# The second layer's modulation blocks move from TensorE to VectorE

## The chip, the cores and the metric

The kernel runs on one core of one Trainium2 chip. The metric is the device time of one execution in microseconds (us), the median of the runs shown. TensorE multiplies matrices into eight PSUM banks, VectorE and ScalarE do elementwise work, SyncE only issues the loads of the weights. Everything lies in fp32; a large product is made of three fp32r products of a rounded high part and a remainder.

## What is computed

The reference is two blocks of two transformer layers on 512 tokens (and 256 context tokens in the first) of 1024 features. For the change the first block's modulation and its first feed-forward part matter:

```
sh1, sc1, g1, sh2, sc2, g2 = ada_modulation(c, w_ada[i], b_ada[i])            # the same for c_ctx
h = modulate(x, norm_mix[i], sh1, sc1)
...
x = x + g2[:, None, :] * conv_ffn(modulate(x, norm_ffn[i], sh2, sc2),
                                  ffn_w_up[i], ffn_conv_w[i], ffn_conv_b[i], ffn_w_down[i])

def conv_ffn(h, w_up, conv_w, conv_b, w_down):
    u = depthwise_conv3(h @ w_up, conv_w, conv_b)
    a, g = jnp.split(u, 2, axis=-1)
    return (jax.nn.silu(g) * a) @ w_down
```

The modulation of layer i is silu(c) and silu(c_ctx), each a vector of 1024, times w_ada[i] (1024 x 6144), plus a bias. It is cut into twelve blocks c of 512 columns. Those of the second layer (i = 1) are needed only from the end of the first feed-forward part on.

## The kernel before

Features lie on partitions, tokens along them: a tile is 128 features by 256 tokens (context) or 512 (main), the "small" and the "large" tile. Each engine runs a list written out by hand, with waits on counts of the others' work (pe_done, act_done, dve_done).

**Weights.** All weights pass a ring of four slots of 128 x 2048 in the order of the list `plan`. SyncE issues the load of piece i when the piece i - 4 has been used: released by VectorE for the pieces that are split, by TensorE for the others. A split piece is rounded by ScalarE (L354, WH), and VectorE takes the remainder (L362, WL); there are two buffers for that, so piece k waits for TensorE to be done with piece k - 2. Up weights are 1 MB in two transfers of 512 KB, down weights 768 KB a half, modulation weights 1 MB a half.

**The stage a0** (the first feed-forward stage, `conv_ffn_*` and `ffn_pe` with the tag "a0") has 22 up blocks j in groups of three (the last group has one). Up group 0 runs first, then up group g and down group g - 1 alternate, and down group 7 ends it. An up block is 2 parts x 2 tiles x 8 x 3 matmuls (`up_pe`, L400) into four banks. ScalarE takes them out with the middle tap of the convolution (L1293), VectorE adds the two others (L1314, L1318), ScalarE applies Silu (L1299), VectorE multiplies (L1325), ScalarE rounds the result (L1273) and VectorE takes its remainder (L1279). A down group is 8 pairs of a small and a large tile of 9 matmuls each (`down_pe`), and VectorE adds each tile to X (L1369). `take` hands out six PSUM banks in turn; a bank is free when its last reader is done. Behind the last down group's tiles a norm follows (L530, L519, L582, L568).

**The modulation blocks of the second layer** hang on the odd up blocks (`extra`, ada1_pe, ada1_act, ada1_dve). `ada_pe` makes 16 products of 256 columns (L627, printed as 32 records) of the weights with the two conditions in the stationary place, in four quarters of the rows of one bank; ScalarE copies the bank to `spare` (L643); `ada_turn_pe` (L635) turns and adds it with four products of two columns (8 records), and VectorE adds the bias (L649). Block 10 stands behind up block 21, and behind it block 11 and the turns of 10 and 11.

Of the kernel before, what the change touches and what calls it, by code (L numbers as in the profile page):

```python
# [109 lines left out]
def build(nc, io, counts):  # L110
    known = counts.known
    ctx = ExitStack()
    with ctx:
# [11 lines left out]
        sel = sb("sel", [P, 2])  # L125
        modv = sb("modv", [P, 2, 48, 2])
# [93 lines left out]
        plan = []  # L220
        GATE_ORDER = [(0, 0), (2, 0), (1, 0), (0, 1), (2, 1), (1, 1)]
# [9 lines left out]
        def weights_list():  # L231
            def ada(l, c):
                pieces(("ada", l, c), io["w_ada"][l], 512 * c, 512 * c + 512)

            for c in range(4):
                ada(0, c)
            g_in = io["gla_w_in"][0]
            for h in range(GLA_H):
                piece((("gla_in", h), 0), [(0, cols(g_in, h * 128, h * 128 + 128)),
                                           (128, cols(g_in, 512 + h * 128, 640 + h * 128))])  # L240
                piece((("gla_in", h), 1), [(0, cols(g_in, 1024 + h * 256, 1280 + h * 256))])
                ada(0, 4 + 2 * h)
# [5 lines left out]
            def ffn(tag, up, down, extra):  # L248
                def ups(g):
                    for j in range(GROUP * g, min(GROUP * g + GROUP, FT)):  # L250
                        piece(("up", tag, j), [(0, cols(up, 128 * j, 128 * j + 128)),
                                               (128, cols(up, FF + 128 * j, FF + 128 * j + 128))], True)
                        if j % 2:
                            extra(j // 2)

                def downs(g):
                    rows = down[128 * GROUP * g:128 * min(GROUP * g + GROUP, FT), :]
                    pieces(("down", tag, g), rows, 0, D, True, 512)

                for g in range(-(-FT // GROUP)):  # L260
                    ups(g)
                    if g:
                        downs(g - 1)
                downs(FT // GROUP)

            def ada1(c):
                ada(1, c)
                if c == FT // 2 - 1:
                    ada(1, c + 1)

            ffn("a0", io["ffn_w_up"][0], io["ffn_w_down"][0], ada1)
# [10 lines left out]
            ffn("a1", io["ffn_w_up"][1], io["ffn_w_down"][1], lambda c: None)  # L282
            for l in range(2):
                w = io["w_in_2"][l]
                piece(("idx", l, 0), [(0, cols(w, 4608, 4864))], True)

                piece(("idx", l, 1), [(0, cols(w, 4864, 4928)), (64, cols(w, 4864, 4932))], True)
                for b in (0, 2, 1):
                    for n in range(3):
                        c0 = 1536 * b + 512 * n  # L290
                        pieces(("in", l, b, n), w, c0, c0 + 512, True)
                for b, c in GATE_ORDER:
                    u = ("w_up_a_2", "w_up_b_2", "w_up_c_2")[b]
                    for i in range(2):
# [8 lines left out]
                ffn(f"b{l}", io["w_gu_2"][l], io["w_down_2"][l], lambda c: None)  # L303

        weights_list()
        where = {}
# [190 lines left out]

        def residual_tiles(spec):
# [11 lines left out]
        def square_act(spec, i):  # L510
# [4 lines left out]
            if i >= 2:  # L515
                nc.scalar.wait_ge(pe_done, at(("hsq_read", key, i - 2)))
            elif ("ada_turned", 1, 10 + i) in counts.at and key == "n1":
                nc.scalar.wait_ge(pe_done, at(("ada_turned", 1, 10 + i)))
# [120 lines left out]
        def ada_act(l, c):  # L639
            nc.scalar.wait_ge(pe_done, at(("ada", l, c)))  # L640
            if c >= 2:
                nc.scalar.wait_ge(pe_done, at(("ada_turned", l, c - 2)))
            nc.scalar.copy(ada_rows[:, c % 2, :], bank_of(("ada", l, c))).then_inc(  # L643
                act_done, mark("act", ("ada_rows", l, c), ("free", ("ada", l, c))))

# [130 lines left out]
        def start_dve():  # L776
            nc.vector.memset(eps[:, :], EPS).then_inc(dve_done, mark("dve", ("eps",)))
            nc.vector.memset(cond[:, :, :], 0.0).then_inc(dve_done, mark("dve", ("cond0",)))
# [431 lines left out]
        GROUPS = -(-FT // GROUP)  # L1210

        def group(g):
            return range(GROUP * g, min(GROUP * g + GROUP, FT))

        def up_pe(tag, groups, g, extra, spec):
            for j in group(g):
# [13 lines left out]
                if j % 2:  # L1230
                    extra(j // 2)
# [8 lines left out]
        def down_pe(tag, groups, g, spec):  # L1240
# [19 lines left out]
        def ffn_pe(tag, groups, extra, spec, out_spec):  # L1260
            for g in range(GROUPS + 1):
                if g < GROUPS:
                    up_pe(tag, groups, g, extra, spec)
# [19 lines left out]
        def conv_act(tag, l, groups, g, extra):  # L1283
            for j in group(g):
# [16 lines left out]
                if j % 2:  # L1301
                    extra(j // 2)

        def conv_dve(tag, l, groups, g, extra):
            for j in group(g):
                split_dve(after(("up", tag, j)))
                for part in range(2):
                    t = 22 * part + j
                    for t0, tn in groups if j else reversed(groups):
# [10 lines left out]
                            ALU.mult, ALU.add).then_inc(dve_done, mark("dve", ("conv", tag, j, part), ("free", key)))  # L1320
                nc.vector.wait_ge(act_done, at(("silu", tag, j)))
# [6 lines left out]
                if j % 2:  # L1328
                    extra(j // 2)
# [43 lines left out]
        def down_dve(tag, groups, g, gate, spec):  # L1373
            for i in range(2):
                split_dve(after((("down", tag, g), i)))
                for n in range(4 * i, 4 * i + 4):
                    for t0, tn in groups:
                        down_tile_add_dve(tag, g, n, t0, tn, gate, spec)

# [36 lines left out]
        def conv_ffn_act(tag, l, groups, extra, spec):  # L1416
            for g in range(GROUPS + 1):
                if g < GROUPS:
                    conv_act(tag, l, groups, g, extra)
# [5 lines left out]
        def conv_ffn_dve(tag, l, groups, gate, extra, spec):  # L1425
            for g in range(GROUPS + 1):
                if g < GROUPS:
                    conv_dve(tag, l, groups, g, extra)
# [1313 lines left out]
        def ada1_pe(c):  # L2742
            ada_pe(1, c)
            if c:
                ada_turn_pe(1, c - 1)
            if c == FT // 2 - 1:
                ada_pe(1, c + 1)
                ada_turn_pe(1, c)
                ada_turn_pe(1, c + 1)

        def ada1_act(c):
            ada_act(1, c)
            if c == FT // 2 - 1:
                ada_act(1, c + 1)

        def ada1_dve(c):
            if c:
                ada_dve(1, c - 1)
            if c == FT // 2 - 1:
                ada_dve(1, c)  # L2760
                ada_dve(1, c + 1)

        def nothing(c):
            pass

# [22 lines left out]
        def _(pe):  # L2788
# [8 lines left out]
            residual_pe("gla_out", lambda k, t0, tn: Y[:, k, t0:t0 + tn], ALL, hnorms["n0f"],  # L2797
                        passes=[(("gla_out", CTX), ALL[1:]), (("gla_out", 0), ALL[:1])])
            ffn_pe("a0", ALL, ada1_pe, hnorms["n0f"], hnorms["n1"])
# [4 lines left out]
            ffn_pe("a1", MAIN, nothing, hnorms["n1f"], hnorms["m", 0])  # L2804
            for l in range(2):
# [16 lines left out]
                ffn_pe(f"b{l}", MAIN, nothing, hnorms["f", l], hnorms["final"] if l else hnorms["m", 1])  # L2822

        @block.scalar
        def _(act):
# [11 lines left out]
            conv_ffn_act("a0", 0, ALL, ada1_act, hnorms["n1"])  # L2837
# [6 lines left out]
            conv_ffn_act("a1", 1, MAIN, nothing, hnorms["m", 0])  # L2844
# [26 lines left out]
        def _(dve):  # L2871
# [11 lines left out]
            conv_ffn_dve("a0", 0, ALL, mod_gate(0, 1), ada1_dve, hnorms["n1"])  # L2883
# [6 lines left out]
            conv_ffn_dve("a1", 1, MAIN, mod_gate(1, 1), nothing, hnorms["m", 0])  # L2890
# [88 lines left out]
```

## Time and profile before

| | us |
|---|---|
| median of 3 runs | 4456.69 |
| lowest, highest | 4453.78, 4457.04 |
| the profiled execution | 4463.18 |
| its span | 4461.4 |
| TensorE busy in the span | 4143.4 (93%) |
| VectorE busy | 1902.6 (43%) |
| ScalarE busy | 1359.2 (30%) |
| mean granted clock of TensorE | 0.959 of full |

The profile lists instructions by source line. Times are counted from the span's start. "L400 x96" are 96 records of line 400; "[0.91 <-ACT conv L1299]" is idle time of the engine ahead of an instruction, and what ended it. The chain follows the work that ended last back from the end, at each step to what released it.

### The profile page before, as it was taken

How to read it: one execution, taken by the hardware profiler on the slowest of the kernel's cores; microseconds unless marked ns; L12 is line 12 of the kernel's file. 1: busy time of each engine (PE TensorE's matmuls, PEld its weight loads, DVE VectorE, ACT ScalarE, POOL GpSimd, SP SyncE). 2: the span in 40 equal slices, each digit the busy share in tenths (PEclk: the TensorE clock that was granted, in tenths of full speed). 3: DMA queues.
4: the chain of work that ended last, by engine and by line, in shares of the span. 5: the costliest groups of instructions: out<-in, count | busy, mean ns of one | idle time of the engine just before them, and what ended most of it. 6: DMA issues, size and time to landing. Idle time of an engine off the chain costs nothing.

```text
span 4461.4 us, 47797 instructions
## 1 busy us (share of the span) xinstructions
PE 4143.4 (93%) x19512; PEld 3053.1 (68%) x19512; DVE 1902.6 (43%) x2995; ACT 1359.2 (30%) x2239; POOL 16.9 (0%) x33
## 2 busy tenths in 40 slices
PE   7999889999988999999888999899988889998999
PEld 3676548888865556887756666588866665656887
DVE  1333115544442325655475531343437754224334
ACT  2222124222234424333133332332222334323222
POOL 0000000000000000000000000000000000000000
PEclk9898999999989999999889999999989999999999
DMA  4232023323220012333111112233232111222331
GB/s 152 67 92 69 29 65 110 109 88 108 89 82 16 26 36 80 96 99 94 60 57 41 55 57 85 69 92 98 82 93 67 50 48 32 82 88 77 96 95 62
DMA packets 385175, 333.51 MB, mean 75 GB/s; under 512 B 12416, under 2 KB 351872, under 8 KB 384832
## 3 DMA queue, kind: packets, MB, share of 16 engines
q1 hardware_dynamic: 382384, 319.09, 23.6%
q0 software_dynamic: 2576, 11.37, 0.8%
q8 instruction: 157, 2.57, 0.2%
q14 instruction: 58, 0.48, 0.0%
HBM read 328.34 MB, written 2.10 MB: 74 GB/s over the span
## 4 chain that ended last, share of the span: by engine, by line
PE 73%; DVE 7%; ACT 5%; issue 2%; DMA 0%; ACTq 0%; DVEq 0%
PE ps L400 53%; PE ps L411 3%; PE ps L413 3%; PE ps L412 3%; PE ps L530 2%; DVE WL L362 1%; ACT WH L354 1%; PE ps L2041 1%; ACT arena_m L1706 1%; PE ps L1666 1%; PE ps L2019 1%; DVE arena_m L1688 1%; DVE arena_m L1683 1%; PE ps L599 1%; PE ps L600 1%
## 5 line engine op out<-in xcount | busy, mean ns | idle before, releaser
L362 DVE TENSOR_TENSOR WL<-ring,WH 128x2048 fp32r<-128x2048 f32 (+3 forms) x221 | 461.3, 2088 | 356.7 <-ACT WH L354 356.4
L354 ACT CAST WH<-ring 128x2048 fp32r<-128x2048 f32 (+3 forms) x221 | 384.1, 1738 | 478.0 <-PE ps L400 386.9
L400 PE MATMUL ps<-MH,WH 128*128 128x512 f32 x1024 | 399.9, 391 | 3.2 <-DVE WL L362 3.2
L400 PE MATMUL ps<-ML,WH 128*128 128x512 f32 x1024 | 399.7, 390 | 0.0
L400 PE MATMUL ps<-MH,WL 128*128 128x512 f32 x1024 | 399.5, 390 | 0.0
L411 PE MATMUL ps<-MH,WH 128*128 128x512 f32 x768 | 344.4, 448 | 13.1 <-DVE WL L362 13.1
L400 PE MATMUL ps<-IH,WH 128*128 128x512 f32 (+1 forms) x880 | 336.9, 383 | 0.0
L400 PE MATMUL ps<-IL,WH 128*128 128x512 f32 (+1 forms) x880 | 325.8, 370 | 0.0
L400 PE MATMUL ps<-IH,WL 128*128 128x512 f32 (+1 forms) x880 | 325.1, 369 | 0.0
L413 PE MATMUL ps<-MH,WL 128*128 128x512 f32 x768 | 310.2, 404 | 0.0
L412 PE MATMUL ps<-ML,WH 128*128 128x512 f32 x768 | 309.8, 403 | 0.0
L400 PE MATMUL ps<-arena_m,ring 128*128 128x512 f32 x640 | 286.0, 595 | 3.3 <-issue 3.3
L400 PE MATMUL ps<-HH,WH 128*128 128x512 f32 (+1 forms) x728 | 246.5, 339 | 0.0
L400 PE MATMUL ps<-HL,WH 128*128 128x512 f32 (+1 forms) x728 | 245.6, 337 | 0.0
L400 PE MATMUL ps<-HH,WL 128*128 128x512 f32 (+1 forms) x728 | 245.1, 337 | 0.0
L400 PEld LDWEIGHTS ps<-MH,WH 128*128 128x128 f32 x1024 | 192.9, 188 | 43.9 <-DVE WL L362 3.6
L400 PEld LDWEIGHTS ps<-ML,WH 128*128 128x128 f32 x1024 | 192.9, 188 | 40.3
L400 PEld LDWEIGHTS ps<-MH,WL 128*128 128x128 f32 x1024 | 192.9, 188 | 40.1
L400 PEld LDWEIGHTS ps<-arena_m,ring 128*128 128x128 f32 x640 | 121.7, 191 | 138.6 <-issue 134.9
L411 PEld LDWEIGHTS ps<-MH,WH 128*128 128x128 f32 x768 | 150.6, 196 | 85.9 <-issue 44.4
L400 PE MATMUL ps<-H,ring 128*128 128x256 f32 (+1 forms) x512 | 185.0, 518 | 10.8 <-ACT arena_a L1123 10.8
L1293 ACT ACTIVATE conv<-ps,vec 128x512 f32<-128x512 f32 (+1 forms) x132 | 92.4, 705 | 321.0 <-PE ps L400 315.4
(289 smaller groups left out, 6808.0 us busy)
## 6 DMA issues: line engine op xcount, KB each, us to landing
ring<-in_w_in SPq DMA_DIRECT2D x62, 1024.0 KB, 5.2
ring<-in_w_ada SPq DMA_DIRECT2D x48, 1024.0 KB, 8.6
ring<-in_ffn_w_up SPq DMA_DIRECT2D x88, 512.0 KB, 5.2
ring<-in_w_gu SPq DMA_DIRECT2D x88, 512.0 KB, 5.1
ring<-in_ffn_w_down SPq DMA_DIRECT2D x28, 768.0 KB, 4.5
ring<-in_w_down SPq DMA_DIRECT2D x28, 768.0 KB, 4.4
ring<-in_gla_w_in SPq DMA_DIRECT2D x8, 1024.0 KB, 9.5
ring<-in_gla_w_out SPq DMA_DIRECT2D x8, 1024.0 KB, 5.0
```

The lines of the kernel that those rows point to most:

```text
L354: nc.scalar.copy(split_slot(key, WH), raw_slot(key)).then_inc(act_done, mark("act", ("rounded", k)))
L362: nc.vector.tensor_tensor(split_slot(key, WL), raw_slot(key), split_slot(key, WH).bitcast(F32), ALU.subtract).then_inc(dve_done, mark("dve ...
L400: m = nc.tensor.matmul(out, l, r, start=(i == 0), stop=(i == len(pairs) - 1))
L411: nc.tensor.matmul(out, lh, rh, start=first and i == 0, stop=False)
L412: nc.tensor.matmul(out, lh, rl, start=False, stop=False)
L413: m = nc.tensor.matmul(out, ll, rh, start=False, stop=end)
L530: m = nc.tensor.matmul(ps[:, bank, 0:tn], mat("mean1024"), NSQ[:, i % 2, 0:tn], start=(n == 0), stop=(n == DT - 1))
L599: nc.tensor.matmul(out, wh, xh, start=(k == 0), stop=False)
L600: nc.tensor.matmul(out, wl, xh, start=False, stop=False)
L1293: nc.scalar.activation(conv[:, j % 2, part, t0:t0 + tn], bank_of(key)[:, 0:tn], ACT.Identity, scale=v("conv_w", 132 * l + 44 + t), bias=v( ...
L1666: m = nc.tensor.matmul(out[64 * e:64 * e + 64, 0:P], it["v"](k)[:, 64 * e:64 * e + 64], pt[:, e, 128 * k:128 * k + 128], start=(k == 0), s ...
L1683: nc.vector.tensor_tensor(probs(i), src, bias, ALU.add).then_inc(dve_done, mark("dve", (name, "biased", i), *[("free", (name, "s", i, e)) ...
```

## The change

The twelve modulation blocks of the second layer leave TensorE. VectorE multiplies each 128 x 512 tile k (0 to 7) of a block's weights by the condition's value of that row and adds it up in `spare`, for the two conditions (s = 0, 1): one TENSOR_SCALAR for k = 0, a SCALAR_TENSOR_TENSOR for each other k (`ada_part_dve`). TensorE then sums the 128 partitions with eight products of one column against a tile of ones (`ada_sum_pe`). The pieces of weights are cut by rows (tiles 0 to 3 and 4 to 7, 512 columns) and their slots are released by VectorE. Blocks 0, 1, 3, 5, 7, 9, 11 lie in up groups 0 to 6 (tiles 0-2, 3-5 and 6-7 in the three up blocks), blocks 2, 4, 6, 8, 10 in down groups 0 to 4 (one tile behind each pair of additions). The sums of the blocks from the ups stand behind the fourth tile of the next down group on TensorE, those from the downs behind the first up block of the next group.

```diff
@@ weights_list
             def ffn(tag, up, down):
                 def ups(g):
                     for j in group(g):
                         piece(("up", tag, j), [...], True)
-                        if j % 2:
-                            extra(j // 2)
+                        if tag == "a0" and g in ADA_UP and j % GROUP < 2:
+                            ada_rows_of(ADA_UP[g], j % GROUP)
                 def downs(g):
-                    pieces(("down", tag, g), rows, 0, D, True, 512)
+                    for i in range(2):
+                        piece((("down", tag, g), i), [(0, cols(rows, 512 * i, 512 * i + 512))], True)
+                        if tag == "a0" and g in ADA_DOWN:
+                            ada_rows_of(ADA_DOWN[g], i)
@@
+        def ada_part_dve(c, ks):
+            if ks[0] == 0:
+                if c == 0:
+                    for t0 in (0, CTX):
+                        nc.vector.wait_ge(pe_done, at(("hms", "n0f", t0)))
+                else:
+                    nc.vector.wait_ge(pe_done, at(("ada_turned", 1, c - 1)))
+                    ada_dve(1, c - 1)
+            for k in ks:
+                key = (("ada", 1, c), k // 4)
+                n, loads_n = where[key]
+                nc.vector.wait_ge(slot_loaded[n % SLOTS], loads_n)
+                x = raw_slot(key).rearrange("p (t n) -> p t n", n=512)[:, k % 4, :]
+                for s in range(2):
+                    acc = ada_sums[:, s, :]
+                    if k == 0:
+                        m = nc.vector.tensor_scalar(acc, x, cond[:, k, s:s + 1], None, ALU.mult)
+                    else:
+                        nc.vector.wait_ge(dve_done, at(("ada_part", c, k - 1, s)))
+                        m = nc.vector.scalar_tensor_tensor(acc, x, cond[:, k, s:s + 1], acc, ALU.mult, ALU.add)
+                    m.then_inc(dve_done, mark("dve", ("ada_part", c, k, s), *([used(key)] if k % 4 == 3 else []),
+                                              *([("ada_sum", c)] if k == DT - 1 else [])))
+
+        def ada_sum_pe(c):
+            nc.tensor.wait_ge(dve_done, at(("ada_sum", c)))
+            out = take(("ada_turned", 1, c))
+            for j in range(4):
+                for s in range(2):
+                    m = nc.tensor.matmul(out[:, 2 * j + s:2 * j + s + 1], ada_sums[:, s, 128 * j:128 * j + 128], ones[:, :],
+                                         start=True, stop=True)
+            m.then_inc(pe_done, mark("pe", ("ada_turned", 1, c)))
@@ up_pe
-                if j % 2:
-                    extra(j // 2)
+                if tag == "a0" and j % GROUP == 0 and j and g - 1 in ADA_BEFORE_UP:
+                    ada_sum_pe(ADA_BEFORE_UP[g - 1])
@@ down_pe
                     done += 1
+                    if tag == "a0" and done == 4 and g in ADA_BEFORE_DOWN:
+                        ada_sum_pe(ADA_BEFORE_DOWN[g])
@@ conv_dve, behind the two convolution instructions of the block's last tile
+                if tag == "a0" and g in ADA_UP:
+                    ada_part_dve(ADA_UP[g], ((0, 1, 2), (3, 4, 5), (6, 7))[j % GROUP])
                 nc.vector.wait_ge(act_done, at(("silu", tag, j)))
@@ down_dve
                     for t0, tn in groups:
                         down_tile_add_dve(tag, g, n, t0, tn, gate, spec)
+                    if tag == "a0" and g in ADA_DOWN:
+                        ada_part_dve(ADA_DOWN[g], (n,))
@@ block.sync
-                if i >= SLOTS and plan[i - SLOTS][2]:
+                if i >= SLOTS and (plan[i - SLOTS][2] or plan[i - SLOTS][0] in summed_pieces):
                     sp.wait_ge(dve_done, at(("slot_used", i - SLOTS)))
```

**SyncE's queue from up block 7 to up block 9, around down group 1.** `in_w_ada` are modulation weights, `in_ffn_w_up` and `in_ffn_w_down` the up and down weights; in brackets is the engine that releases the slot. Before:

```order
L2780 DMA ring<-in_ffn_w_up 128x8x128 [waits pe_done]
L2780 DMA ring<-in_ffn_w_up 128x8x128
L2780 DMA ring<-in_w_ada 128x8x256 [waits dve_done] x2
L2780 DMA ring<-in_ffn_w_up 128x8x128 [waits dve_done]
L2780 DMA ring<-in_ffn_w_up 128x8x128
L2780 DMA ring<-in_ffn_w_down 128x3x512 [waits dve_done]
L2780 DMA ring<-in_ffn_w_down 128x3x512 [waits pe_done]
L2780 DMA ring<-in_ffn_w_up 128x8x128 [waits pe_done]
L2780 DMA ring<-in_ffn_w_up 128x8x128
```

After:

```order
L2808 DMA ring<-in_ffn_w_up 128x8x128 [waits dve_done]
L2808 DMA ring<-in_ffn_w_up 128x8x128
L2808 DMA ring<-in_w_ada 128x4x512 [waits dve_done]
L2808 DMA ring<-in_ffn_w_up 128x8x128 [waits dve_done]
L2808 DMA ring<-in_ffn_w_up 128x8x128
L2808 DMA ring<-in_ffn_w_down 128x3x512 [waits dve_done]
L2808 DMA ring<-in_w_ada 128x4x512 [waits dve_done]
L2808 DMA ring<-in_ffn_w_down 128x3x512 [waits dve_done]
L2808 DMA ring<-in_w_ada 128x4x512 [waits dve_done]
L2808 DMA ring<-in_ffn_w_up 128x8x128 [waits dve_done]
L2808 DMA ring<-in_ffn_w_up 128x8x128
```

The halves of a modulation block now stand apart, one behind each of two up weights and one behind each half of the down weights, and every slot is released by VectorE.

**VectorE from the third up block of a group into the first pairs of the down group.** `conv` is the convolution's result, `WL` the remainder of the weights, `spare` the sums of a modulation block, `modv` its result. Before:

```order
L1314 SCALAR_TENSOR_TENSOR conv<-ps,vec,conv 128x511
L1318 SCALAR_TENSOR_TENSOR conv<-ps,vec,conv 128x511
L1325 TENSOR_TENSOR conv<-conv 128x768
L1279 TENSOR_TENSOR IL<-conv,IH 128x768
L649 TENSOR_TENSOR modv<-ps,vec 128x4 x2
L362 TENSOR_TENSOR WL<-ring,WH 128x1536
L1369 SCALAR_TENSOR_TENSOR X<-ps,modv,X 128x256
L1369 SCALAR_TENSOR_TENSOR X<-ps,modv,X 128x512
L1369 SCALAR_TENSOR_TENSOR X<-ps,modv,X 128x256
L1369 SCALAR_TENSOR_TENSOR X<-ps,modv,X 128x512
```

After:

```order
L1362 SCALAR_TENSOR_TENSOR conv<-ps,vec,conv 128x511
L1366 SCALAR_TENSOR_TENSOR conv<-ps,vec,conv 128x511
L680 SCALAR_TENSOR_TENSOR spare<-ring,cond,spare 128x512 x4
L1375 TENSOR_TENSOR conv<-conv 128x768
L1329 TENSOR_TENSOR IL<-conv,IH 128x768
L372 TENSOR_TENSOR WL<-ring,WH 128x1536
L1417 SCALAR_TENSOR_TENSOR X<-ps,modv,X 128x256
L1417 SCALAR_TENSOR_TENSOR X<-ps,modv,X 128x512
L697 TENSOR_TENSOR modv<-ps,vec 128x4 x2
L677 TENSOR_SCALAR spare<-ring,cond 128x512 x2
L1417 SCALAR_TENSOR_TENSOR X<-ps,modv,X 128x256
L1417 SCALAR_TENSOR_TENSOR X<-ps,modv,X 128x512
```

Four instructions (tiles 6 and 7 of a block) stand ahead of the product of the up block, and two behind each pair of additions.

**TensorE behind the second pair of a down group**, where the sum stands now:

```order
L410 MATMUL ps<-IH,WH 128x512
L410 MATMUL ps<-IL,WH 128x512
L410 MATMUL ps<-IH,WL 128x512
L690 MATMUL ps<-ones,spare 128x1 x8
L410 MATMUL ps<-IH,WH 128x256
L410 MATMUL ps<-IL,WH 128x256
L410 MATMUL ps<-IH,WL 128x256
```

Before, no down group held anything but its own products; the modulation products stood behind odd up blocks.

## Rows read from the trace of the kernel before

**Rows 1.** The page, part 1: busy time and share of the span by engine.

```profile
PE 4143.4 (93%) x19512; PEld 3053.1 (68%) x19512; DVE 1902.6 (43%) x2995; ACT 1359.2 (30%) x2239; POOL 16.9 (0%) x33
```

**Rows 2.** The chain in order of time: start us, length us, what; stage a0.

```profile
698.75 16.69 PE ps L400 x96
...
1169.81 58.59 PE ps L400 x336
1229.45 4.46 DMA ring<-in_ffn_w_down
...
1248.86 27.55 PE ps L400 x144
```

**Rows 3.** Busy time in a stretch: us, DVE busy, clock, DMA share, GB/s.

```profile
698.00:1228.00 530.00, 262.14 (x354) 1.00 0.33 99
```

**Rows 4.** The chain from 985 to 1075 us, around a modulation block.

```profile
1007.78 1.86 PE ps L627 x32
1009.64 0.98 PE ps L635 x8
1010.63 58.59 PE ps L400 x336
```

**Rows 5.** TensorE behind up block 21: start, us, line; in brackets idle before.

```profile
1228.32 1.93 PE L627 MATMUL ps<-ring,cond 128*32 128x256 f32 x32
...
1238.27 3.64 PE L627 MATMUL ps<-ring,cond 128*32 128x256 f32 x32 [7.03 <-ACT conv L1293]
1245.29 3.58 PE L635 MATMUL ps<-sel,spare 128*128 128x2 f32 x16 [3.38 <-ACT spare L643]
```

**Rows 6.** ScalarE in the same place.

```profile
1233.99 1.47 ACT L354 CAST WH<-ring 128x1536 fp32r<-128x1536 f32 x1 [32.89 <-DMA ring<-in_ffn_w_down]
```

**Rows 7.** VectorE by line and shape: count, busy us, mean ns.

```profile
L582 DVE SCALAR_TENSOR_TENSOR stage_b<-X,gain,stage_b 128x512 f32<-128x512 f32 x24 | 17.6, 744 | 18.6 <-ACT stage_b L540 18.6
...
L1696 DVE TENSOR_SCALAR arena_m<-arena_m 128x512 f32<-128x512 f32 x32 | 14.1, 484 | 0.6
```

**Rows 8.** VectorE, two instructions in a row: start us, us.

```profile
1310.27 0.74 DVE L568 SCALAR_TENSOR_TENSOR HL<-stage_b,modv,HH 128x512 fp32r<-128x512 f32 x1
1310.93 0.74 DVE L582 SCALAR_TENSOR_TENSOR stage_b<-X,gain,stage_b 128x512 f32<-128x512 f32 x1
```

**Rows 9.** VectorE from up block 14 into down group 3.

```profile
1029.05 0.75 DVE L1318 SCALAR_TENSOR_TENSOR conv<-ps,vec,conv 128x511 f32<-128x511 f32 x1
1030.71 0.96 DVE L1325 TENSOR_TENSOR conv<-conv 128x768 f32<-128x768 f32 x1 [0.91 <-ACT conv L1299]
...
1034.01 1.76 DVE L362 TENSOR_TENSOR WL<-ring,WH 128x1536 fp32r<-128x1536 f32 x1 [0.42 <-ACT WH L354]
1035.68 3.63 DVE L1369 SCALAR_TENSOR_TENSOR X<-ps,modv,X 128x256 f32<-128x256 f32 x7
...
1049.43 0.75 DVE L1369 SCALAR_TENSOR_TENSOR X<-ps,modv,X 128x512 f32<-128x512 f32 x1 [1.58 <-PE ps L400]
1050.51 0.48 DVE L1369 SCALAR_TENSOR_TENSOR X<-ps,modv,X 128x256 f32<-128x256 f32 x1 [0.32 <-PE ps L400]
1052.57 0.75 DVE L1369 SCALAR_TENSOR_TENSOR X<-ps,modv,X 128x512 f32<-128x512 f32 x1 [1.58 <-PE ps L400]
```

**Rows 10.** Time from issue to landing of the loads of `in_ffn_w_down`.

```profile
DMA to landing us min/median/max: 2.5/4.4/10.3
```

**Rows 11.** TensorE behind two standstills, at 2900 and at 3277 us.

```profile
2900.58 0.76 PE L599 MATMUL ps<-MH,WH 128*128 128x512 f32 x1 [3.70 <-DVE ML L571]
...
3277.20 0.47 PE L599 MATMUL ps<-MH,WH 128*128 128x512 f32 x1 [3.80 <-DVE ML L571]
```

**Rows 12.** TensorE's clock (behind the busy us) in the stretches that follow.

```profile
2899.00:2903.00 4.00, 2.42 (x6) 0.50 1.02 263
2903.00:2906.00 3.00, 3.00 (x9) 0.53 0.00 0
3277.50:3281.00 3.50, 3.50 (x10) 0.56 0.00 0
```

More of the change, by code:

```diff
@@ L125, in build @@
         sel = sb("sel", [P, 2])
+        ones = sb("ones", [P, 1])
         modv = sb("modv", [P, 2, 48, 2])
@@ L220, in build, with group @@
         plan = []
+        GROUPS = -(-FT // GROUP)
+        ADA_UP = {0: 0, 1: 1, 2: 3, 3: 5, 4: 7, 5: 9, 6: 11}
+        ADA_DOWN = {g: 2 * g + 2 for g in range(5)}
+        def group(g):
+            return range(GROUP * g, min(GROUP * g + GROUP, FT))
         GATE_ORDER = [(0, 0), (2, 0), (1, 0), (0, 1), (2, 1), (1, 1)]
@@ L246, in weights_list, with ada_rows_of, ffn @@
             pieces(("gla_out", 0), io["gla_w_out"][0], 0, D)
-            def ffn(tag, up, down, extra):
+            def ada_rows_of(c, i):
+                piece((("ada", 1, c), i), [(0, cols(io["w_ada"][1][512 * i:512 * i + 512, :], 512 * c, 512 * c + 512))])
+            def ffn(tag, up, down):
                 def ups(g):
-                    for j in range(GROUP * g, min(GROUP * g + GROUP, FT)):
+                    for j in group(g):
                         piece(("up", tag, j), [(0, cols(up, 128 * j, 128 * j + 128)),
                                                (128, cols(up, FF + 128 * j, FF + 128 * j + 128))], True)
-                        if j % 2:
-                            extra(j // 2)
+                        if tag == "a0" and g in ADA_UP and j % GROUP < 2:
+                            ada_rows_of(ADA_UP[g], j % GROUP)
                 def downs(g):
                     rows = down[128 * GROUP * g:128 * min(GROUP * g + GROUP, FT), :]
-                    pieces(("down", tag, g), rows, 0, D, True, 512)
+                    for i in range(2):
+                        piece((("down", tag, g), i), [(0, cols(rows, 512 * i, 512 * i + 512))], True)
+                        if tag == "a0" and g in ADA_DOWN:
+                            ada_rows_of(ADA_DOWN[g], i)
                 for g in range(-(-FT // GROUP)):
@@ L264, in ffn @@
                 downs(FT // GROUP)
[L266 to L271, printed above, removed]
+            ffn("a0", io["ffn_w_up"][0], io["ffn_w_down"][0])
             dn = io["mla_w_down"][0]
@@ L302, in weights_list @@
                 piece(("xo", l), [(0, cols(io["w_o_x_2"][l], 0, 1024))])
-                ffn(f"b{l}", io["w_gu_2"][l], io["w_down_2"][l], lambda c: None)
+                ffn(f"b{l}", io["w_gu_2"][l], io["w_down_2"][l])
         weights_list()
+        summed_pieces = [(("ada", 1, c), i) for c in range(12) for i in range(2)]
         where = {}
@@ L496, in norm_buffers @@
             return late_tiles if spec[0] == "n0f" else (NF, NR)
+        GLA_OUT = [(("gla_out", CTX), ALL[1:]), (("gla_out", 0), ALL[:1])]
         def residual_tiles(spec):
@@ L516, in square_act @@
                 nc.scalar.wait_ge(pe_done, at(("hsq_read", key, i - 2)))
-            elif ("ada_turned", 1, 10 + i) in counts.at and key == "n1":
-                nc.scalar.wait_ge(pe_done, at(("ada_turned", 1, 10 + i)))
+            elif key == "n1":
+                nc.scalar.wait_ge(pe_done, at(("ada_turned", 1, 11)))
             nc.scalar.activation(NSQ[:, i % 2, 0:tn], X[:, n, t0:t0 + tn], ACT.Square).then_inc(
@@ L1208, in gla_dve, with up_pe @@
                 gla_y_dve(n, i)
[L1210 to L1215, printed above, removed]
+        ADA_BEFORE_UP = {0: 0, 1: 2, 2: 4, 3: 6, 4: 8, 5: 10}
+        ADA_BEFORE_DOWN = {0: 1, 1: 3, 2: 5, 3: 7, 4: 9, 5: 11}
+        def up_pe(tag, groups, g, spec):
             for j in group(g):
@@ L1258, in down_pe, with ffn_pe @@
                     mean_pe(spec, i)
-        def ffn_pe(tag, groups, extra, spec, out_spec):
+        def ffn_pe(tag, groups, spec, out_spec):
             for g in range(GROUPS + 1):
                 if g < GROUPS:
-                    up_pe(tag, groups, g, extra, spec)
+                    up_pe(tag, groups, g, spec)
                 if g:
@@ L1281, in rest_inter_dve, with conv_act @@
                                         dve_done, mark("dve", ("inter", tag, j)))
-        def conv_act(tag, l, groups, g, extra):
+        def conv_act(tag, l, groups, g):
             for j in group(g):
@@ L1300, in conv_act, with conv_dve @@
                 round_inter_act(tag, j, groups[0][0])
-                if j % 2:
-                    extra(j // 2)
-        def conv_dve(tag, l, groups, g, extra):
+        def conv_dve(tag, l, groups, g):
             for j in group(g):
@@ L1378, in down_dve @@
                         down_tile_add_dve(tag, g, n, t0, tn, gate, spec)
+                    if tag == "a0" and g in ADA_DOWN:
+                        ada_part_dve(ADA_DOWN[g], (n,))
+                    elif tag == "a0" and g == 5 and n == 1:
+                        ada_dve(1, 11)
         def last_down_act(tag, g, spec):
@@ L1414, in last_down_dve, with conv_ffn_act @@
             hnorm_dve(spec, between)
-        def conv_ffn_act(tag, l, groups, extra, spec):
+        def conv_ffn_act(tag, l, groups, spec):
             for g in range(GROUPS + 1):
                 if g < GROUPS:
-                    conv_act(tag, l, groups, g, extra)
+                    conv_act(tag, l, groups, g)
                 if g == GROUPS and spec[0] == "n1":
@@ L1423, in conv_ffn_act, with conv_ffn_dve @@
                     down_act(tag, groups, g - 1, spec)
-        def conv_ffn_dve(tag, l, groups, gate, extra, spec):
+        def conv_ffn_dve(tag, l, groups, gate, spec):
             for g in range(GROUPS + 1):
                 if g < GROUPS:
-                    conv_dve(tag, l, groups, g, extra)
+                    conv_dve(tag, l, groups, g)
                 if g == GROUPS and spec[0] == "n1":
@@ L2739, in subln_gain_dve @@
             nc.vector.wait_ge(dve_done, at(("sg", l)))
[L2742 to L2764, printed above, removed]
         block = ctx.enter_context(nc.Block())
@@ L2796, in _ @@
             meet("pe", pe, "gla_norm")
-            residual_pe("gla_out", lambda k, t0, tn: Y[:, k, t0:t0 + tn], ALL, hnorms["n0f"],
-                        passes=[(("gla_out", CTX), ALL[1:]), (("gla_out", 0), ALL[:1])])
-            ffn_pe("a0", ALL, ada1_pe, hnorms["n0f"], hnorms["n1"])
+            residual_pe("gla_out", lambda k, t0, tn: Y[:, k, t0:t0 + tn], ALL, hnorms["n0f"], passes=GLA_OUT)
+            ffn_pe("a0", ALL, hnorms["n0f"], hnorms["n1"])
             latent_pe()
@@ L2803, in _ @@
             norm_pe(norms["mem"], 6)
-            ffn_pe("a1", MAIN, nothing, hnorms["n1f"], hnorms["m", 0])
+            ffn_pe("a1", MAIN, hnorms["n1f"], hnorms["m", 0])
             for l in range(2):
@@ L2821, in _ @@
                 residual_pe(("xo", l), lambda k, t0, tn: XO[:, k, :], MAIN, hnorms["f", l], [(("xo", l), 0, 8)])
-                ffn_pe(f"b{l}", MAIN, nothing, hnorms["f", l], hnorms["final"] if l else hnorms["m", 1])
+                ffn_pe(f"b{l}", MAIN, hnorms["f", l], hnorms["final"] if l else hnorms["m", 1])
         @block.scalar
@@ L2836, in _ @@
             gla_out_act(hnorms["n0f"])
-            conv_ffn_act("a0", 0, ALL, ada1_act, hnorms["n1"])
+            conv_ffn_act("a0", 0, ALL, hnorms["n1"])
             latent_act()
@@ L2843, in _ @@
             rstd_act(norms["mem"], 0)
-            conv_ffn_act("a1", 1, MAIN, nothing, hnorms["m", 0])
+            conv_ffn_act("a1", 1, MAIN, hnorms["m", 0])
             ln_exp_tables()
@@ L2882, in _ @@
             gla_out_dve(mod_gate(0, 0), hnorms["n0f"])
-            conv_ffn_dve("a0", 0, ALL, mod_gate(0, 1), ada1_dve, hnorms["n1"])
+            conv_ffn_dve("a0", 0, ALL, mod_gate(0, 1), hnorms["n1"])
             latent_dve()
@@ L2889, in _ @@
             norm_dve(norms["mem"])
-            conv_ffn_dve("a1", 1, MAIN, mod_gate(1, 1), nothing, hnorms["m", 0])
+            conv_ffn_dve("a1", 1, MAIN, mod_gate(1, 1), hnorms["m", 0])
             for l in range(2):
```

6 lines of the change are left out of this document (3 added, 3 removed).

## The prediction

> **What bounds the kernel now.** I read four views in this order. The page's totals first: TensorE is busy 93% of the span, VectorE 43% [rows 1]. Then the chain of work that ended last, in order of time: through the stage a0 (the first feed-forward stage, 681 to 1277 us) it is nothing but matmuls of L400, broken eleven times by modulation work. One up block is 96 records in 16.7 us; a down group is 144 records in 25.1 us (58.59 less two up blocks) [rows 2]. So until 1228.4 us a0 costs what TensorE is given to do, and VectorE, busy 262 of 530 us [rows 3], has room on average. Third, the chain around a modulation block, for what it costs TensorE [rows 4]. Fourth, TensorE and ScalarE behind the last up block, where alone TensorE stands still [rows 5, 6].
>
> **What goes.** (1) A modulation block in mid-stage takes TensorE 1.86 us for the products and 0.98 us for the turn of the block before it, 2.84 us [rows 4]; there are nine like it, and the first has no turn: 9 x 2.84 + 1.86 = 27.4 us. All of it is on the path. (2) The tail: up block 21 ends at 1228.4, down group 6 begins at 1248.86 and takes 27.55 us instead of 25.1 [rows 2]. In between stand blocks 10 and 11, three turns, and two waits [rows 5]: a ring slot is freed for the next down weights only when block 10 is used (issued 1229.45, landed 4.46 us later), ScalarE rounds them (it had waited 32.89 us for them [rows 6]) before it touches the up block's output, and block 11 waits for a bank held by that output. The 2.4 us more in the group are its start at the lower clock. After the change nothing stands between up block 21 and down group 6: its weights' slot was freed by up block 20, its hidden tiles are older than up block 21. I count 20.5 + 2.4 = 22.9 us as gone. What is late next is the narrow part behind down group 7, which is left as it is. Together 50.3 us go. ScalarE's twelve copies go too; they were off the path and count nothing.
>
> **What TensorE gets.** Twelve sums of eight one-column products. The turn is the nearest row: four products, printed as eight records, 0.98 us; sixteen records took 3.58 us at half clock [rows 5], that is 1.8 us at full. With the entry I take 2.1 us (1.8 to 2.4): 12 x 2.1 = 25.2 us. Were there nothing else, the gain would be 25.1 us.
>
> **What VectorE gets.** Per block 2 TENSOR_SCALAR and 14 SCALAR_TENSOR_TENSOR over 128x512. The trace has both with all operands in SBUF: 484 and 744 ns, and SCALAR_TENSOR_TENSORs in a row start 0.66 us apart [rows 7, 8]. With 0.40 for the first kind a block is 2 x 0.40 + 14 x 0.66 = 10.0 us, twelve 121 us. 262 + 121 = 383 of some 530 us: on average it fits. Each of a dependent pair has the other token set's instruction between, so I add no bubble. The Vector Engine (DVE) Microarchitecture Reference of the Trainium skill ("Points that are easy to get wrong") says that a SCALAR_TENSOR_TENSOR with two SBUF sources that are not bf16 runs at half throughput. By that the blocks would cost some 90 us more; the 744 ns of L582, which reads two fp32 tiles of SBUF, speak against it.
>
> **Up blocks.** Let T be the end of an up block on TensorE. VectorE's last convolution instruction ends at T+2.4 (T is 1027.4, one up block behind 1010.63 [rows 4]; the instruction is that of 1029.05 [rows 9]). Six added instructions (3.5 to 4.0 us) then stand ahead of the product L1325, in part in its old wait of 0.9 us. The rounded tile, ScalarE's rounding of the next weights (1.9 us) and VectorE's remainder (2.3 us) follow it and end near T+12.3; TensorE wants them at T+16.7. The banks are free in time. Cost nothing, cover 4.4 us.
>
> **Down groups: the new wait.** Here the order of the queue decides. In groups 1 to 5 the loads run: up, M0, up, M1, up, D0, m0, D1, m1 (M: a modulation block's halves, D: the down weights' halves). The ring has four slots, so D1 takes M1's slot, and that is freed by VectorE's last instruction on k=7, in the third up block's part. Before, such a slot was freed by TensorE long ahead. Worked out from [rows 9]: convolution ends 1029.7; four instructions of 0.66 end at 1032.45; D1 is issued at 1032.5 and lands 4.46 later (4.4 is the median of such loads, 10.3 the longest [rows 10]), 1037.0; ScalarE's rounding starts VectorE's 1.5 us later, 1038.55; the remainder of the weights takes 1.67 to the first addition, 1040.2 instead of 1035.68. The bank of the first small tile is free at 1040.7.
> When does TensorE want it? Small tile 1.08, large tile 2.06, so 3.14 us per pair [rows 9]. Six banks go round. The last up block holds four, two are free; its part 0 is long read. The sum takes a bank of its own behind the second pair, so that the third pair's large tile, not the fourth's small one, is the first to need a bank of the first pair: at 1027.4 + 6.3 + 2.1 + 1.1 = 1036.8. TensorE stands still 1040.7 - 1036.8 = 3.9 us, five times (down groups 0 to 4): 19.5 us. In down group 5 no modulation block lies between, D1's slot is an up block's; only the four instructions delay it, less the old wait of 0.9: the additions begin at T+10.0, the bank is free at T+10.5 instead of T+9.5, 1.0 us. Bounds: nothing (if the banks or the load were no limit), and 5 us each if D1 shares the engines with the two loads queued right behind it. Behind the stall VectorE needs 1.07 + 1.33 = 2.4 us per pair against TensorE's 3.14 and catches up; it ends its part some 3 us into the next up block, whose weights are then still early.
>
> **The clock.** In dense work a standstill of 3.70 and one of 3.80 us were each followed by a granted clock of 0.50 (1.2 instead of 2.4 GHz): in the one case from 2899 to about 2905.9, 5.2 us of them worked, 2.6 us lost; in the other 3.1 us of 3.5, 1.6 lost [rows 11, 12]. So five standstills of 3.9 us cost another 1.6 to 2.6 each; I take 2.2, 11.0 us.
>
> **The sum.** Added 25.2 + 19.5 + 1.0 + 11.0 = 56.7, removed 50.3: 6.4 us slower. Against the profiled execution's own 4463.2 us that is 4469.6; the median of the runs is 4456.7, 6.5 below it, and I forecast 4463.1.
>
> **The rivals.** (A) The wait is not there: D1 lands in time or the banks are enough. For it: VectorE's average load and the loads' slack elsewhere. Then 50.3 - 25.2 less at most 6 x 1.0 = 19 to 25 us faster, about 4435. Against it: the slot rule is in the program's order, and before the change the additions already begin only 0.6 us ahead of need. 0.18. (B) The standstills come, but the clock holds: 45.7 added, 4.6 us faster, 4452. Against it: both rows of a standstill this long. 0.17. (C) VectorE becomes the bound: its added instructions take longer than L582's, because they read the ring slots while transfers write others. At 1.2 us each, a pair costs it 1.07 + 2.4 = 3.5 us against 3.14, and the four ahead of D1 2.2 us more: (2.2 + 8 x 0.35) x 5 = 25 us more than the forecast, 4488. It decides from about 1.0 us an instruction, where a pair costs VectorE what it costs TensorE. Against it: 744 ns. 0.10. (The Trainium skill's rule on two SBUF sources, above, would lead here too.) That the change does nothing of what it says is excluded by the order of instructions. The forecast itself has 0.55, its own range 4452 to 4474 (standstills of 3 to 5 us, clock 1.6 to 3.1 each, sums 1.8 to 2.4).
>
> **How the numbers follow.** A measurement of this kernel can tell about 0.2%, 8.9 us, from no change. Faster by more (below 4447.8): A, with a little of B: 0.20. Slower by more (above 4465.6): C and somewhat over a third of the forecast: 0.31. Within: 0.49. The range is 4436 to 4475: it holds the forecast's own, B and about half of A, and leaves out C.
>
> **What would show it.** In the changed kernel's chain: up blocks in 16.7 us, twelve gaps of about 2.1 us at L690, and no standstill between up block 21 and down group 6. In the waits: TensorE's L410 idle five times some 4 us on VectorE in mid down group, ScalarE's L364 rounding D1 waiting for its load, the granted clock at 0.5 behind each. SCALAR_TENSOR_TENSOR at L680 near 745 ns. Wrong would be: no such waits (A), a clock of 1.00 (B), L680 above 1 us or TensorE waiting in the up blocks too (C).

## The result, and the profile after

| | before | after |
|---|---|---|
| median of 20 runs | 4449.74 us | 4460.44 us |
| the profiled execution | 4463.18 us | 4460.43 us |
| its span | 4461.4 us | 4458.6 us |
| stage a0, up block 1 to the start of down group 7 | 577.7 us | 584.2 us |

The ratio is 1.0023, with a 95% interval of 1.0016 to 1.003: the change makes the kernel 7 to 13 us slower. The forecast was 6.4 us slower. The two profiled executions stand the other way round; the difference lies outside the stage, and more is said of it below (both kernels once more). The stage is read from the chain in both profiles.

The page's first part of the changed kernel, the answer to [rows 1]: TensorE has 18 us less to do and VectorE 115 us more.

```profile
PE 4125.1 (93%) x19224; PEld 3054.0 (68%) x19224; DVE 2017.2 (45%) x3188; ACT 1353.7 (30%) x2227; POOL 16.9 (0%) x33
```

The chain of the changed kernel in order of time (start, length, what), the answer to [rows 2]:

```profile
690.61 50.05 PE ps L410 x288
742.34 33.49 PE ps L410 x192
780.88 4.84 DMA ring<-in_ffn_w_down
789.50 36.80 PE ps L410 x195
827.98 33.49 PE ps L410 x192
866.51 4.83 DMA ring<-in_ffn_w_down
...
1122.64 4.74 DMA ring<-in_ffn_w_down
1131.18 36.63 PE ps L410 x195
1169.49 33.49 PE ps L410 x192
1213.40 61.43 PE ps L410 x339
```

Where before only matmuls and modulation products stood, a load of down weights now lies on the chain once in every down group from 0 to 4, five times. The last row runs through up block 21 and down group 6 without a break: the tail of [rows 5] is gone.

One of the five in detail, the chain from 1015 to 1065 us:

```profile
1036.56 0.76 DVE spare L680
...
1037.34 4.61 DMA ring<-in_ffn_w_down
...
1042.02 1.48 ACT WH L364
...
1043.53 0.04 DVE WL L372
...
1045.20 0.49 DVE X L1417
...
1045.73 19.33 PE ps L410 x96
```

Read from the top: the four added instructions end, their slot is free, the load is issued (1037.34) and lands 4.61 us later, ScalarE rounds it, VectorE takes the remainder, adds the first small tile, and TensorE goes on. VectorE in the same place, the answer to [rows 9]:

```profile
1034.58 2.73 DVE L680 SCALAR_TENSOR_TENSOR spare<-ring,cond,spare 128x512 f32<-128x512 f32 x4
...
1043.53 1.76 DVE L372 TENSOR_TENSOR WL<-ring,WH 128x1536 fp32r<-128x1536 f32 x1 [3.44 <-ACT WH L364]
```

Who waited in a0 (engine, line, for whom: us in total, times, longest):

```profile
PE ps L410 <- DVE X L1417: 23.5, 6, 4.5
...
ACT WH L364 <- DMA ring<-in_ffn_w_down: 17.6, 10, 3.2
```

The granted clock behind that standstill (stretch, us, busy, clock), the answer to [rows 12]:

```profile
1041.00:1045.00 4.00, 0.42 (x4) 0.78 1.07 378
1045.00:1050.00 5.00, 4.27 (x11) 0.50 0.57 141
1050.00:1055.00 5.00, 5.00 (x31) 0.99 0.01 3
```

And the prices of what was added, the answer to [rows 7]:

```profile
L680 DVE SCALAR_TENSOR_TENSOR spare<-ring,cond,spare 128x512 f32<-128x512 f32 x168 | 115.8, 745 | 0.0
L690 PEld LDWEIGHTS ps<-ones,spare 128*128 128x128 f32 x192 | 23.3, 191 | 0.9
L690 PE MATMUL ps<-ones,spare 128*128 128x1 f32 x192 | 22.1, 245 | 0.0
L677 DVE TENSOR_SCALAR spare<-ring,cond 128x512 f32<-128x512 f32 x24 | 10.5, 478 | 0.0
```

### The profile page after: what moved, and what is told of

Its sections match the earlier page's. It is cut to its first block, busy times and chain, and to the rows that moved or that the text cites. A ratio compares the mean times of both kernels' runs of the same rounds, so it can differ in the third digit from the quotient of the medians.

```text
span 4458.6 us, 47486 instructions
## 1 busy us (share of the span) xinstructions
PE 4125.1 (93%) x19224; PEld 3054.0 (68%) x19224; DVE 2017.2 (45%) x3188; ACT 1353.7 (30%) x2227; POOL 16.9 (0%) x33
## 4 chain that ended last, share of the span: by engine, by line
PE 72%; DVE 7%; ACT 5%; issue 2%; DMA 1%; DVEq 0%; ACTq 0%
PE ps L410 53%; PE ps L421 3%; PE ps L423 3%; PE ps L422 3%; PE ps L542 2%; ACT WH L364 1%; PE ps L2093 1%; DVE WL L372 1%; ACT arena_m L1758 1%; PE ps L1718 1%; PE ps L2071 1%; DVE arena_m L1740 1%; DVE arena_m L1735 1%; PE ps L611 1%; PE ps L612 1%
## 5 line engine op out<-in xcount | busy, mean ns | idle before, releaser
L410 PEld LDWEIGHTS ps<-IH,WH 128*128 128x128 f32 x880 | 169.2, 192 | 58.6 <-DVE X L1417 25.0
```

The source lines that it names most:

```text
L410: m = nc.tensor.matmul(out, l, r, start=(i == 0), stop=(i == len(pairs) - 1))
```

## The experiments

The theory: the second half of the down weights (D1) gets a ring slot that VectorE frees only with the modulation block's last tile, so it lands late, the additions behind it are late, and TensorE meets that at a bank. The rivals: the four instructions alone, or VectorE's load as such, make the standstill; or TensorE waits for the weights themselves. In every run the stage was read from the chain as above; the medians are given beside it, and each ratio is that of the run to the kernel before.

### The order of the loads

```diff
                     for i in range(2):
                         piece((("down", tag, g), i), [...], True)
+                    for i in range(2):
                         if tag == "a0" and g in ADA_DOWN:
                             ada_rows_of(ADA_DOWN[g], i)
```

> The changed kernel with one edit in the order of the loads: in down groups 0 to 4 the two halves of the down weights are issued first (D0, D1), then the two halves of the modulation block. D1 so takes the slot of an up block, freed long before, and the modulation half takes the slot that VectorE frees last. Theory (D1's slot is freed late, so D1 lands late, so the additions and a bank are late): D1 is in the ring in time, only the four VectorE instructions ahead of it delay it, as in down group 5 of the changed kernel; the five standstills fall from some 4.4 us to some 1.3 us, the granted clock falls for a shorter time or not at all, and the kernel is 16 to 27 us faster than the changed one, that is 5 to 16 us faster than the kernel before. Rival (the four instructions and VectorE's load make the standstill, not the slot): the standstills stay at 4.4 us and the kernel stays some 10 us above the kernel before.

Measured: 4445.9 us, ratio to before 0.9986 (0.9977 to 0.9995). The stage takes 564.2 us, 20.0 less than in the changed kernel. TensorE's waits in a0:

```profile
PE ps L411 <- DVE X L1418: 7.7, 6, 1.3
```

Six waits of 1.3 us at most, where there had been five of 4.3 to 4.5. The load has left the chain, the four instructions are still where they were: of a standstill 3.1 us were the slot's, and 1.3 are left to the instructions. The rival that the instructions alone make the whole standstill falls. The clock fell all the same behind four of the six standstills; the pieces of the chain tell its price:

```profile
790.68 34.72 PE ps L411 x195
...
871.00 37.45 PE ps L411 x195
```

The same 195 matmuls; the stretches of these two pieces show the clock at full and at 0.92:

```profile
790.68:825.40 34.72, 34.72 (x198) 1.00 0.58 171
871.00:908.45 37.45, 37.45 (x198) 0.92 0.53 158
```

That is 2.7 us for the clock, the most of the four (the others 1.4 to 1.6). In the changed kernel the same piece took 36.6 to 36.8 us, 2.0 us for the clock.

### The block earlier on VectorE

```diff
-                if tag == "a0" and g in ADA_UP:
-                    ada_part_dve(ADA_UP[g], ((0, 1, 2), (3, 4, 5), (6, 7))[j % GROUP])
+                if tag == "a0" and g in ADA_UP and j % GROUP < 2:
+                    ada_part_dve(ADA_UP[g], ((0, 1, 2, 3), (4, 5, 6, 7))[j % GROUP])
```

> The changed kernel with one edit on VectorE: in an up group all eight tiles of the modulation block are added up in the first two up blocks (tiles 0 to 3, tiles 4 to 7), none in the third. Same instructions, same loads, same sums. Theory: the slot that D1 takes is freed one up block (16.7 us) earlier and nothing stands ahead of the additions, so all six standstills of the down groups vanish with the low clock behind them: 22.2 + 1.3 us of standstills and some 12.8 us of clock, 36 us faster than the changed kernel, 26 us faster than the kernel before. Eight instructions (5.3 us) in an up block push the remainder of the next weights to T+13.6 of 16.7 us, no wait. Rival (VectorE's total load is the bound): as much work as before in all, so no gain, or new waits of TensorE in the first two up blocks, since each carries 1.3 us more.

Measured: 4432.57 us, ratio 0.9958 (0.9946 to 0.9969). The stage takes 547.7 us, 36.6 less than in the changed kernel, as the theory had it (36). No wait of TensorE is left in it; the chain is matmuls broken by sums alone (two pieces of it):

```profile
741.20 39.76 PE ps L410 x228
782.64 35.63 PE ps L410 x204
```

741.20 + 39.76 = 780.96, and the next piece starts at 782.64: a sum costs 1.68 us. VectorE does exactly the same instructions as in the changed kernel, so its total load is not what cost the time. The median is 28 us below the changed kernel's, not 36: the stage behind (below).

### The same run again

> The kernel in which an up group's modulation block is done in its first two up blocks, repeated. Its stage was 30 us shorter than the kernel before's, its median 19 us below (0.9946 to 0.9969). If the 11 us between are chance in the rest of the kernel, this median lies nearer to 4424; if not, 19 us again.

Measured: 4437.67 us, ratio 0.9958 (0.9946 to 0.9971); the stage takes 547.66 us both times. The stage is again 30 us shorter than the kernel before's. The median is 14 us below that of the kernel before in the same experiment (4451.74 us), the ratio says 19. By either, at least 11 us of the stage's gain do not reach the whole, for the second time.

### The block later on VectorE

```diff
-                    ada_part_dve(ADA_UP[g], ((0, 1, 2), (3, 4, 5), (6, 7))[j % GROUP])
+                    ada_part_dve(ADA_UP[g], ((0, 1), (2, 3), (4, 5, 6, 7))[j % GROUP])
```

> The changed kernel with the opposite edit: of a modulation block in an up group, tiles 0-1 in the first, 2-3 in the second and 4-7 in the third up block, so that eight instead of four instructions stand ahead of the release of the slot that D1 takes. Theory: each release is 4 x 0.66 = 2.65 us later, and so is each standstill: five of 7.1 us, and 1.3 + 2.65 us in down group 5, 16 us slower than the changed kernel, 26 us slower than the kernel before, less if the low clock falls more into the standstill. Rival (the standstill hangs on the transfer's own time or on the banks alone): no change against the changed kernel.

Measured: 4487.39 us, ratio 1.0082 (1.007 to 1.0094). The stage takes 604.1 us, 19.9 more than in the changed kernel, where 16 were expected. The direction is the theory's, and the size has a part that it lacked:

```profile
PE ps L410 <- DVE X L1417: 29.1, 6, 6.5
PE ps L690 <- DVE spare L680: 8.7, 6, 1.5
```

With eight instructions in the third up block the sum itself comes too early: TensorE now waits for VectorE there (1.5 us), and again at the bank (4.4 to 6.5 us in down groups 0 to 4, where 7.1 were expected without the wait at the sum). The load is issued as late as expected. Sum and bank together are 5.9 to 8.0 us of standstill in a group, and the clock fell for longer: over 15 us around a standstill it is 0.66 to 0.68 here (first row), 0.77 in the changed kernel (second).

```profile
782.00:797.00 15.00, 9.14 (x45) 0.66 0.63 192
```

```profile
785.00:800.00 15.00, 10.50 (x45) 0.77 0.44 136
```

### More banks

```diff
         turn = [0]
+        banks = [6]
...
-                bank = turn[0] % 6
+                bank = turn[0] % banks[0]
...
         def ffn_pe(tag, groups, spec, out_spec):
             for g in range(GROUPS + 1):
+                banks[0] = 8 if tag == "a0" and 1 <= g <= 6 else 6
```

> The changed kernel with eight instead of six PSUM banks handed out in turn from up group 1 to down group 5; loads and VectorE's order are as in the changed kernel, so D1 lands as late as there. Theory (D1 late, therefore the additions late, therefore a bank late, and TensorE meets it at the bank): two more banks put off TensorE's need by one pair, 3.14 us, so the five standstills fall from 4.3-4.6 to about 1.2-1.4 us and that of down group 5 vanishes; the stage is 19 us shorter, up to 30 us if the clock stays up behind them, and the kernel 9 to 19 us faster than before. Rival (TensorE waits for the weights D1 themselves): the standstill only moves to the fifth pair, and nothing is gained.

Measured: 4434.55 us, ratio 0.9963 (0.9949 to 0.9976). The stage takes 555.4 us, 28.8 less than in the changed kernel. D1 is on the chain as late as ever, but its lateness costs little:

```profile
779.03 4.69 DMA ring<-in_ffn_w_down
787.52 31.58 PE ps L411 x177
```

```profile
PE ps L411 <- DVE X L1419: 6.4, 5, 1.3
```

177 records instead of 195 lie behind the standstill: it moved by 18 records, one pair of tiles, and shrank from 4.4 to 1.3 us. So TensorE waited for the bank and not for the weights. Here the clock stayed up behind all five (one of the five stretches):

```profile
786.00:797.00 11.00, 9.73 (x57) 1.00 0.34 83
```

### The tail with the blocks on TensorE

This run starts from the kernel before, with all blocks still on TensorE. Its edit puts blocks 0 to 11 behind the up blocks of the list ADA_AT, `[1, 3, 5, 7, 9, 11, 13, 15, 16, 17, 18, 19]`, and the last turn behind up block 20:

```diff
-                if j % 2:
-                    extra(j // 2)
+                extra(j)
...
+        def ada1_pe(j):
+            if j in ADA_AT:
+                ada_pe(1, ADA_AT.index(j))
+            if j in ADA_AT[1:]:
+                ada_turn_pe(1, ADA_AT.index(j) - 1)
+            if j == 20:
+                ada_turn_pe(1, 11)
```

> The kernel before, modulation blocks still on TensorE, but the last ones earlier: blocks 0 to 6 stay behind up blocks 1, 3 to 13, and blocks 7 to 11 stand behind up blocks 15 to 19, the last turn behind 20, so that nothing stands behind up block 21. Theory (20.5 us between up block 21 and down group 6 and 2.4 us of low clock come from the blocks that stood there, of which 2 x 2.84 us come back in mid-stage): 17 us faster than the kernel before. Rival (the tail is bound by the loads or by the convolution in any case): no faster than the kernel before, and the changed kernel's tail would be its only gain that needs VectorE.

Measured: 4440.45 us, ratio 0.9975 (0.9966 to 0.9984). The stage takes 561.6 us, 16.1 less than before (17 expected). Up block 20's end to down group 7 is one piece:

```profile
1193.36 67.05 PE ps L400 x384
```

The products of blocks 10 and 11 and three turns, 2 x 1.86 + 3 x 0.98 = 6.7 us, are now paid in mid-stage, and 16.1 + 6.7 is 22.8 us, the whole of the tail. (The 17 counted two turns coming back; there are three.) So the tail's cost was the blocks' place and not their engine: the larger part of what the change gains there can be had without VectorE.

### Both kernels once more

> The kernel before, unchanged, for a second profile. Between the profiles so far the code ahead of the stage (0 to 690 us) and behind it, which is the same in all of them, took 3874 to 3886 us in sum, with 95 us of low clock ahead of the stage in some and 119 us in others. If that is chance from run to run, this profile's rest differs from the first profile of the same kernel by as much (up to 10 us) and the median stays at that of the kernel before; if it hangs on the kernel, stage a0 begins at 698.8 us and the rest is 3884 us again.

> The changed kernel, unchanged, in the same call. Stage a0 from up block 1 to the start of down group 7 takes 584 us again with five standstills of 4.3-4.6 us at the same places, 6.6 us more than the kernel before; the median is 6 to 13 us above the kernel before. If the rest of the kernel varies by chance, the stage stays and the start of the stage moves by up to 9 us against the first profile.

Measured: before 4453.7 us (1.0004, 0.9995 to 1.0013), after 4462.34 us (1.0022, 1.0013 to 1.0031). The stages take 576.9 and 582.6 us. The start of the stage moved from 698.8 to 692.6 us in the kernel before, and the time of all that is not the stage from 3883.7 to 3874.1 us. The two profiled executions of this one kernel differ by 10.4 us (4463.18 and 4452.77), and 9.6 of them lie ahead of and behind the stage. So it is no effect of the change that the first profile of before is longer than that of the changed kernel. In the second changed kernel the five standstills are there again:

```profile
PE ps L410 <- DVE X L1417: 23.3, 6, 4.5
```

## Why the prediction was right, step by step

- **The tail.** Held. 22.9 us were counted as gone; in the changed kernel's chain nothing stands there, and e4_before_spread takes it away by moving the blocks alone (16.1 us net, 22.8 with what it pays elsewhere).
- **What TensorE no longer does in mid-stage** (27.4 us). Held; the matmuls between are the same, up block pairs of 33.5 us.
- **The sums.** Mis-sized: 1.68 us each instead of 2.1, 20.2 instead of 25.2 us. The allowance for the entry was wrong, and even the low end of the stated 1.8 to 2.4 us was too high.
- **VectorE's price.** Held: 745 and 478 ns against 744 and 484. The Trainium skill (Vector Engine (DVE) Microarchitecture Reference, "Points that are easy to get wrong") says that a SCALAR_TENSOR_TENSOR with two SBUF sources that are not bf16 runs at half throughput. The trace does not agree: the 168 instructions at L680 took 740 to 751 ns each, and those of this size in the kernel before that read one source from PSUM 746 to 750 on average.
- **Up blocks cost nothing.** Held, and e2_early shows that even 1.3 us more per block are covered. In e3_late, with up to eight instructions in one block, two loads of up weights came onto the chain at the start of the stage.
- **The new wait.** Held in place, number and cause: five times in down groups 0 to 4, and a small one in group 5. Size 4.3 to 4.5 us against 3.9: the load took 4.6 to 4.8 us instead of 4.46 (two more are issued right behind it; whether they slow it was not tried), and the shorter sum lets TensorE reach the bank 0.4 us earlier. 22.2 us instead of 19.5, and 1.3 instead of 1.0. e1_swap shows the slot's part, e5_banks8 the bank's.
- **The clock.** Held: 0.50 behind each of the five, 2.0 us each against 2.2, and 1.6 us once behind the small standstill (61.43 us for the last piece, 59.85 in the second profile, where the clock stayed up there), where I had counted none. As a sum 11.4 against 11.0.
- **The sum.** 20.2 + 22.2 + 1.3 + 11.4 is 55.1 us added; the stage says 57. The difference lies at the standstills: from one sum behind an up block to the next, over a down group and three up blocks, the chain takes 85.3 to 85.6 us, where the matmuls (3 x 16.74 + 25.1) and two sums make 78.7, so a standstill and its clock cost 6.6 to 6.9 us, 0.2 to 0.5 more than the two rows say. 56.7 was forecast with 6.1 for each. That the total fits is luck of the terms: the sums were 5.0 us too dear, the six standstills with their clock 5.3 too cheap. The stage lost 6.6 and 5.7 us in the two pairs of profiles.
- **The kernel.** By its medians it lost 10.7 us. That is 4.3 us more than forecast. In the two pairs of profiles the changed kernel takes 2.4 and 4.5 us longer between the end of the stage and a1, a part that the forecast took as unchanged; the cause stays open. The forecast time of 4463.1 us is closer to the measured 4460.44 than that, by luck: it started from a median of three runs, 4456.69, which is 7 us above the median of 20. One bound was added up wrong: with the ends given for the terms (5 us, 3.1 and 2.4) the forecast's own range ends at 4476.7, not at 4474.

Rival A (no wait) is refuted by the waits, rival B (the clock holds) by the clock, rival C (VectorE the bound) by 745 ns and by e2_early. The clock did stay up five times in e5_banks8, but behind standstills of 1.3 us, not of 4.

Each of two small edits to the changed kernel beats both kernels: the block in the first two up blocks (0.9958 of before, twice), or eight banks (0.9963). The last two tiles of a block stood in the wrong place. Whether the work should be on VectorE at all is a comparison with e4_before_spread, which keeps it on TensorE: in the stage VectorE wins by 13.9 us (547.7 against 561.6), but the ratios of the whole kernel, 0.9958 and 0.9975, have intervals that touch, so there it is not settled.

## What to carry to other kernels

In a ring of slots the question is not only what an instruction costs its engine, but what it holds: a weight consumed late by a slow reader delays the load that takes its slot, and that load's readers. Follow each new reader's last instruction to the load that it releases, and count from there to the bank or tile that the bound engine needs next. A standstill costs more than its length: here 4.4 us brought 2.0 more by the clock.

## What the runs showed of the hardware

**The clock behind short standstills.** Behind the standstills of 4.3 to 4.5 us the clock fell every time, ten times in two profiles. Behind those of 1.3 us it fell five times out of thirteen: in four of six in e1_swap, in none of five in e5_banks8, and behind the one in down group 5 in the first profile of the changed kernel but not in the second, though the program is the same (first and second profile; stretch, us, busy, clock):

```profile
1213.00:1218.00 5.00, 4.60 (x17) 0.66 0.96 355
```

```profile
1213.00:1218.00 5.00, 3.70 (x22) 1.00 1.07 352
```

So a standstill of 1.3 us has no fixed price here; what decides it no run shows.

**A later stage that nobody touched.** The stages behind a0 are the same instructions in every kernel here, and yet they did not take the same time. From the start of the latent projections to the first large piece of a1 (stretch, us, busy, clock; in this order before, before again, after, e2_early, e8_early_again, e5_banks8):

```profile
1321.57:1725.44 403.87, 366.14 (x1549) 0.97 0.12 35
```

```profile
1314.63:1718.10 403.47, 363.49 (x1549) 0.97 0.12 35
```

```profile
1321.26:1726.26 405.00, 366.28 (x1548) 0.97 0.12 35
```

```profile
1283.95:1695.06 411.11, 371.21 (x1549) 0.95 0.11 34
```

```profile
1282.39:1693.50 411.11, 371.18 (x1548) 0.95 0.11 34
```

```profile
1292.16:1694.00 401.84, 363.52 (x1549) 0.97 0.11 35
```

The stretch is full of short waits, and the mean granted clock was 0.95 in some kernels and 0.97 in others. It is no chance of one run: both profiles of the early block give 411.11 us, e3_late 410.97, and the two of before 403.5 and 403.9. This is 7 of the 11 us between e2_early's stage and its median; another 1.7 lie between the end of the stage and this stretch (46.8 us against 45.1). What decides it was not tried. So a part of a stage's gain can be lost in a later stage that nobody touched, and a difference of some 7 us in this kernel is no evidence for or against an edit unless its own stage shows it.
